# Two stacked models in float32: most token-to-feature tiles turned by VectorE block transposes and a bounce through a scratch array, in place of TensorE and transposing DMAs

## The reference

```
h   = mlstm_chunkwise(q, k, v, i_pre, log_f)          # 8 heads, matrix memory
y_a = headnorm(h * sigmoid(o)) * g * silu(z_a)
xc  = causal_dwconv(xb, lru_conv_w) + lru_conv_b
r,i = sigmoid(xc @ w_a + b_a), sigmoid(xc @ w_x + b_x)   # blocks of 256x256
log_a = -8 * r * softplus(-lam)
h_t = exp(log_a) * h_(t-1) + xc * i * sqrt(1 - exp(2 * log_a))
y_b = h * silu(z_b)
x   = x + concat(y_a, y_b) @ w_out
```

## Time and profile before

| | |
|---|---|
| median of 3 runs | 3274.63 us (3273.33 to 3274.72) |
| span of the profiled execution, first to last instruction | 3271.3 us |
| its own time beside the span | its span and about 3.3 us around it, by the median |
| TensorE clock granted | 1.000 |
| PE busy | 3257.1 us (100%), 15142 matmuls |
| DVE busy | 2082.9 us (64%) |
| ACT busy | 1830.6 us (56%) |
| POOL busy | 174.0 us (5%) |
| DMA | 637.77 MB, mean 195 GB/s |
| queue of the weight loads | 59.2% of 16 engines' span |

### The profile page before, as it was taken

The page is one execution under the profiler, slowest core; times in us unless marked ns, Lnnn a source line. Parts: engine busy times, 40 slices in busy tenths (PEclk is TensorE's granted clock), DMA queues, the critical chain, the costliest instruction groups (busy, mean ns, idle before and its releaser), DMA issues.

```text
span 3271.3 us, 39485 instructions
## 1 busy us (share of the span) xinstructions
PE 3257.1 (100%) x15142; PEld 2708.7 (83%) x15142; DVE 2082.9 (64%) x2843; ACT 1830.6 (56%) x2394; POOL 174.0 (5%) x241
## 2 busy tenths in 40 slices
PE   9999999999999999999999999999999999999999
PEld 7888888888888888888888888888888888888887
DVE  6558655756757755657667565665555667757664
ACT  5555545546665455546665565555556555565553
POOL 2000000000000000000000000000000321200000
PEclk9999999999999999999999999999999999999999
DMA  8666666565566666565567666556656565575565
GB/s 274 211 205 196 200 194 187 191 192 176 181 208 197 192 195 197 183 201 174 186 211 228 189 206 193 183 176 190 193 185 207 173 183 181 191 228 188 180 198 174
DMA packets 395740, 637.77 MB, mean 195 GB/s; under 512 B 102108, under 2 KB 104484, under 8 KB 395168
## 3 DMA queue, kind: packets, MB, share of 16 engines
q1 hardware_dynamic: 382928, 601.50, 59.2%
q0 software_dynamic: 10336, 27.45, 2.7%
q10 hardware_dynamic: 2288, 6.30, 0.5%
HBM read 608.10 MB, written 6.62 MB: 188 GB/s over the span
## 4 chain that ended last, share of the span: by engine, by line
PE 94%; ACT 2%; DVE 2%; DMA 1%; issue 1%; SPq 0%; ACTq 0%
PE acc L1727 29%; PE acc L1729 29%; PE acc L1728 29%; DVE weights_lo L1272 1%; PE tr L1814 1%; ACT weights_hi L946 1%; PE nm L1917 1%; ACT work L1012 1%; PE tr L1796 0%; PE tr L1727 0%; ACT work L1005 0%; PE tr L1729 0%; PE tr L1905 0%; PE tr L1728 0%; SPq L768 0%
## 5 line engine op out<-in xcount | busy, mean ns | idle before, releaser
L1272 DVE TENSOR_TENSOR weights_lo<-weights_raw,weights_hi 128x1024 fp32r<-128x1024 f32 x1103 | 1340.6, 1229 | 953.3 <-ACT weights_hi L946 950.0
L946 ACT ACTIVATE weights_hi<-weights_raw 128x1024 fp32r<-128x1024 f32 x1103 | 1156.0, 1057 | 1003.4 <-PE acc L1729 919.1
L1727 PE MATMUL acc<-weights_hi,u_hi 128*128 128x512 f32 x3136 | 1237.5, 395 | 0.0
L1729 PE MATMUL acc<-weights_hi,u_lo 128*128 128x512 f32 x3136 | 1222.6, 390 | 0.0
L1728 PE MATMUL acc<-weights_lo,u_hi 128*128 128x512 f32 x3136 | 1221.4, 389 | 0.0
L1727 PEld LDWEIGHTS acc<-weights_hi,u_hi 128*128 128x128 f32 x3136 | 588.9, 188 | 124.7 <-issue 4.0
L1729 PEld LDWEIGHTS acc<-weights_hi,u_lo 128*128 128x128 f32 x3136 | 588.5, 188 | 123.6
L1728 PEld LDWEIGHTS acc<-weights_lo,u_hi 128*128 128x128 f32 x3136 | 589.0, 188 | 119.3
L1727 PE MATMUL acc<-weights_hi,y_hi 128*128 128x512 f32 x1280 | 501.6, 392 | 0.9 <-DVE y_lo L1276 0.3
L1729 PE MATMUL acc<-weights_hi,y_lo 128*128 128x512 f32 x1280 | 498.6, 390 | 0.0
L1728 PE MATMUL acc<-weights_lo,y_hi 128*128 128x512 f32 x1280 | 498.2, 389 | 0.0
(11 more groups left out here) (285 smaller groups left out, 1957.7 us busy)
## 6 DMA issues: line engine op xcount, KB each, us to landing
weights_raw<-in_w_in_dram SPq DMA_DIRECT2D x384, 512.0 KB, 3.9
weights_raw<-in_w_out_dram SPq DMA_DIRECT2D x256, 512.0 KB, 4.4
weights_raw<-in_a_w_in_dram SPq DMA_DIRECT2D x176, 512.0 KB, 4.2
weights_raw<-in_b_w_in_dram SPq DMA_DIRECT2D x112, 512.0 KB, 3.7
weights_raw<-in_c_w_in_dram SPq DMA_DIRECT2D x112, 512.0 KB, 4.3
weights_raw<-in_w_mem_kv_dram SPq DMA_DIRECT2D x63, 512.0 KB, 5.1
kv_scratch<-work ACTq DMA_DIRECT2D x8, 512.0 KB, 5.3
qk_tiles<-in_w_a_dram POOLq DMA_DIRECT2D x8, 512.0 KB, 4.4
```

What stands on the lines that cost most here:

```text
L946: SC_E.activation(WH[:, b % RING], RAW[:, b % RING], ACT.Copy).then_inc(sem("hi_done"), 1)
L1272: V.tensor_tensor(WL[:, b % RING], RAW[:, b % RING], WH[:, b % RING].bitcast(F32), ALU.subtract).then_inc(sem("lo_done"), 1)
L1727: T.matmul(dst, hi_l, hi_r, start=start, stop=False, **kw)
L1729: return T.matmul(dst, lo_l, hi_r, start=False, stop=stop, **kw)
```

## The change

A turn is now: one DVE instruction transposes all 32x32 blocks of the 256x512 tile (128x1024 elements) into a buffer (piece `flip`); POOL stores that buffer to a scratch array in HBM with four DMAs, one for each 32 partitions, in pieces of 1 KB; three slots later (`fetch`) POOL waits for the four stores and loads the array back as 128 rows of 4 KB, with features on partitions and the tokens of each feature in runs of 32. What reads the tile takes it in that order.

All tiles but 15 take this way: 81 turns (37 of `xbar`'s kind, now `bounce`; 8 q, 8 xb, 8 z_b, 20 queries and keys). Still turned by PE are the memory's four tiles, the first four of x, the fourth tile of x at five layer ends, and the third group of kinds B and C. There are five scratch arrays (lanes), each shared by buffers that aren't in use together. `apart`, the transposing DMAs, `ct` and `cz` are gone. `join` reads the fetched tile directly (four ACT instructions, of 256 elements), `low` is eight DVE instructions of 128 with a gain, or four without, and comes one slot behind `join` instead of two.

Slots move with it. Counted from the end of its chunk, a q or xb tile is flipped at once, joined at +5, convolved at +6 and +7; the gates of the LRU come at +10 and +11 (before: about +6 and +7 from the second round on), the scans at +16 (before +12), `lrz` 8 and `lry` 10 slots behind the z_b chunk (before 5 and 7). `qt` comes 6 slots behind the chunk instead of 3; attention starts at `h - 1` instead of `h - 3` or `h - 4`, the memory's two or three slots later; `ya` is flipped 6 slots behind its z_a chunk (before, taken apart or turned at 8).

```diff
-ISSUE, JOIN, LOW = 7, 5, 2
+FETCH, JOIN, LOW = 3, 5, 1
+LANE = {"u0": "uq", "q": "uq", "a0": "uq", "u1": "um", "m": "um", "x": "xz", "z": "xz", "n": "n",
+        "a": "ab", "b": "ab"}
...
-    def apart(slot, src, ready, buf):
-        q = pl.piece(slot, "apart", src=src, ready=ready, buf=buf)
-        pl.piece(slot + ISSUE, "turn", at=q, buf=buf)
+    def turn(slot, src, ready, buf):
+        q = pl.piece(slot, "flip", src=src, ready=ready, buf=buf)
+        pl.piece(slot + FETCH, "fetch", at=q, buf=buf)
         return q
+    def bounce(slot, src, ready, dst, kt0, gain, buf):
+        q = turn(slot, src, ready, buf)
+        p = pl.piece(slot + JOIN, "join", dst=dst, kt0=kt0, gain=gain, at=q, buf=buf)
+        pl.piece(slot + JOIN + LOW, "low", at=p, buf=buf)
+    def keys_in(hn, **kw):
+        q = turn(pl.here() + 1, "n", ("hn_out", hn), "n")
+        pl.piece(pl.here() + 6, "qt", at=q, buf="n", **kw)
...
+            q = turn(pl.here(), "xt", ("cq_x", cq), "q")
+            pl.piece(pl.here() + 5, "cjoin", at=q, buf="q")
+            for r in range(2):
+                pl.piece(pl.here() + 6 + r, "conv", to="cq", r=r, l=l, taps=QC + 4 * j)
+            pl.piece(pl.here() + 8, "cqs", j=j)
...
-            ya.append(tp(s + 8, "o", ("mf_out", mf), "y", 12, gain) if p == 3 else
-                      xbar(s + 8, "o", ("mf_out", mf), "y", 4 * p, gain, "m"))
+            ya.append(bounce(s + 6, "o", ("mf_out", mf), "y", 4 * p, gain, "m"))
...
-            pl.piece(pl.here() + 1, "ct", to="cx", at=cx)
+            q = turn(pl.here(), "xt", ("cx_x", cx), "x")
+            pl.piece(pl.here() + 5, "cjoin", at=q, buf="x")
...
-            c += 4 if p == 0 else 2
+            c = pl.here() + 7
...
-            pl.piece(pl.here() + 3, "cz", at=zb)
-            pl.piece(pl.here() + 5, "lrz", l=l, p=p)
-            lr.append(pl.piece(pl.here() + 7, "lry", l=l, p=p))
+            q = turn(pl.here(), "xt", ("zb_out", zb), "z")
+            pl.piece(pl.here() + 8, "lrz", l=l, p=p, at=q)
+            lr.append(pl.piece(pl.here() + 10, "lry", l=l, p=p))
...
-            tm = attention("mem", 3, pl.here() - NB + 4)
+            tm = attention("mem", 3, pl.here() - NB + (6 if kind == "A" else 7))
...
-                ts.append(attention(kind, grp, h - 3 if kind == "B" else h - 4))
+                ts.append(attention(kind, grp, h - 1))
...
+        SPILL = {lane: nc.dram_tensor("turn_scratch_" + lane, [4, 32, 4, 256], F32).ap()
+                 for lane in LANES}
...
+                    if k == "flip":
+                        wait(pool, "flipped", p)
+                        for a in range(4):
+                            pool.dma_start(SPILL[LANE[p.buf]][:, :, a].rearrange("b r e -> r b e"),
+                                           flipped(p.buf)[32 * a:32 * a + 32].rearrange("p (b e) -> p b e", b=4)
+                                           ).then_inc(sem("spilled_" + LANE[p.buf]), 16)
+                    elif k == "fetch":
+                        pool.wait_ge(sem("spilled_" + LANE[p.buf]), 64 * (p.nth + 1))
+                        pool.dma_start(turned(p.buf), SPILL[LANE[p.buf]].rearrange("b r a e -> (b r) (a e)")
+                                       ).then_inc(sem("fetched_" + LANE[p.buf]), 16)
...
+                    elif k == "flip":
+                        ref(dve, p.ready)
+                        if p.nth:
+                            dve.wait_ge(sem("fetched_" + LANE[p.buf]), 16 * p.nth)
...
+                        V.transpose(flipped(p.buf).rearrange("p (b q s) -> p q b s", b=4, q=8), src
+                                    ).then_inc(sem("flipped"), 1)
...
                     elif k == "qt":
-                        wait(act, "qt_pe", p)
+                        act.wait_ge(sem("fetched_n"), 16 * (p.at.nth + 1))
...
                     elif k == "lrz":
-                        for j in range(2):
-                            z = ZT[:, 2 * j:2 * j + 2]
-                            i = stt(z, z, 1.0, TR[:, j].rearrange("p (a b) -> p a b", b=256), ALU.add, ALU.mult)
+                        for t in range(2):
+                            for f in range(4):
+                                z = tokens(ZT, t)[:, f]
+                                i = stt(z, z, 1.0, by_token("z", t)[:, f], ALU.add, ALU.mult)
```

244 lines of the change are left out of this document (98 added, 146 removed).

## The result

The changed kernel takes 3533.14 us (median of 4 runs, 3530.86 to 3555.03) beside 3274.47 for the kernel before (4 runs): a ratio of 1.0804 [1.0785, 1.0822], 259 us slower. The forecast was 3318, its range 3256 to 3352. The direction was right and the size was off by a factor of six: +44 forecast, +259 measured.

The account below looks back on a forecast made before the run. PE, busy 3257.1 of 3271.3 us, was taken to bound the kernel; 81 us of new waits (38 + 8 + 10 + 19 + 6) less 37.4 saved gave +44, so 3318 us, range 3256 to 3352.

Parts of the forecast that it names:

- L = 9.1: Each turn, from the end of DVE's transpose to the data's return: 9.1 us, ends 8.0 and 11.
- PE saves 37.4: On PE, 42 of 44 transposed tiles go, at 0.89 us each: 37.4 us saved.
- Stores 3.0, fetch 4.1: Within a turn, a 128 KB store lands in 3.0 us and the fetch takes 4.1 us.
- DMA load at nothing, up to 5 us: 81 x 1 MB moved, 85 MB or 13% more traffic; costs nothing, up to 5 us if landing slows.
- LRU 38: LRU stage, four rounds per layer: DVE's burst and the x turn make PE wait 38 us in two layers.
- q tiles 8: q tiles: the loop through one buffer runs late, 4.2 us per layer with gate rows, 8 in all (4 to 16).
- Last `ya` 10: Last `ya` tile of a layer: ready about 5 us after w_out's block needs it, 10 us in two layers.
- Keys in B and C 19: Attention in kinds B and C: normalization and turns at head groups cost 9.6 us in each kind, 19 in all.
- The lead covers 5.6 us: Weight blocks: a DVE or ACT burst making `weights_lo` up to about 5.6 us late costs nothing.
- rivals, 1 and 4: 1: lead hides the waits, 3237 or 3255 to 3265, chance 0.25. 4: waits cancel the saving, 3275, chance 0.10.
- Rival 3: POOL's DMA issues wait for DVE instructions, lengthening each turn by about 5 us: about 3408 us; chance 0.04.
- Rival 2: The turn is dearer, by a 2.4 us transpose or stores landing in over 4 us: 3349 to 3383; chance 0.11.

Follow-up runs that it names:

- in_place: Changed kernel without the turns' stores and loads, so readers take the DVE-transposed buffer as it stands: 3286.96 us, ratio 1.0035.
- in_place_traffic: Changed kernel with all stores and loads issued, loads going to a spare array, readers taking the transposed buffer without waiting: 3332.21 us, ratio 1.0173.

## Why the prediction was wrong

The step that failed is the sum's term **L = 9.1**, which measured 13.4, and with it the end of 11 that the range was made from; and a term was left out, **the clock**. New waits were 201 us, not 81, the clock cost 78, not 0, and the broken overlap of matmuls some 14 by the estimate above: 120 + 78 + 14 = 212 of the miss of 215. Of the 201, 33 are there in in_place and 30 more in in_place_traffic, by PE's idle time (47.1 and 77.2 us); the 138 that are left come with L. So the traffic and the issues, priced at nothing, are a second part of the step. (Waits below are counted from the usual 0.227 us between starts, so each holds 0.16 us of this overlap.)

- *PE saves 37.4.* Right: L1814's 208 and 104 transposes and L1796's 144 became 120, and PE's busy time fits the saving (-37.4 + 78 + 14, measured +59.8).
- *Transpose 1.22, issue 0.53.* Right (1.236, 0.558).
- *Stores 3.0, fetch 4.1.* Wrong: 5.2 for the fourth store, and 5.8. 3.0 is right for the first store of a turn (2.9) and for every store from SP (2.8 to 3.1); what was priced at nothing is the company of three others on POOL's queue, which the rows of a single 8 KB store and of 16 KB loads don't show. The upper end of 11 was built from the same rows. The fetch was taken below its nearest row (4.4); why it needs 5.8 stays open; it is not POOL's queue, since one from SP beside the same stream needs as long (5.1 to 6.9).
- *DMA load at nothing, up to 5 us.* Wrong: in_place_traffic puts 45 on traffic and issues together, and ACT's waits for weight loads went from 63.8 to 216.6 us. The forecast named these waits as a sign that it would be wrong. Its 39 us for them are two of the five arrays, which are all that the earlier trace rows shows; its 85 MB leave out what the transposing DMAs no longer move, so that the total grew by 64 MB, 10% and not 13%.
- *LRU 38.* Measured 42 (20.1 and 21.9 a layer; gate matmuls 2.4 to 2.85 late for 2.4, the block behind the scans 3.0 for 3.5, since `lrz` took 2.97 for 3.65, the tail 4.1 for 4.75). Right in its places and sizes: the block behind the scans and the tail wait as long in in_place, at L = 0, so they are DVE's burst, as forecast. But L was 12.8 there (transpose's end to `cjoin`, 779.16 to 791.94 in the second round). The 3.7 more did not show; PE itself came later, by 11 us of lower clock per stage (0.05 x 221.8), 2.8 a round. That this is what hid them is argued, not tested. Rounds took 59.6 and 57.9 us between `x` transposes, for a forecast of 55.
- *q tiles 8.* Measured 34. With 4.3 more of L in each of three loops the same walk gives 4.2 + 12.9 = 17.1 a layer, 34 in two. That it fits so well is in part luck: in_place, with L = 0, waits 4.1 a layer in the same stretch, which the walk doesn't have, and 4.6 are the gate rows, which wait for weights behind POOL's stores and not for a q tile. Kind A's memory query fits by L alone: 6 forecast, 14 measured, 2 x (2.9 + 4.3) = 14.4.
- *Last `ya` 10.* Measured 29 with the rest of the v, o and z_a chunks. The two waits for the last tile's `y_lo` are 7.9 and 7.8 of it: 16 where 10 were forecast, a little less than two times 4.3 more. The other 13 stand at `weights_lo` of blocks before, where the forecast had none; what held those up was not traced.
- *Keys in B and C 19.* Measured 70 (28 and 42). Six late points times 4.3 and the 19 give 45. The remaining 25 are most likely the bias loads behind POOL's stores in kind C, where in_place_traffic is 20 longer than in_place; that is argued, not separated. The forecast put `fc` there, and did not name the bias loads. *Memory keys 0*: measured 7.
- *The lead covers 5.6 us.* It holds where DVE is late once. A join that waits on ACT holds up the three splits behind it, and the lead is used up at once: "behind it stand the next split" was written of DVE's transpose and not of ACT's join, the one that waits longest.

Of the rivals, 1 and 4 fall by the time itself, and in_place, with L = 0, is still not faster. Rival 3 falls, although L did grow by about the 5 us that it priced: the 281 issues with DVE busy for over 90% of them took 0.559 us in the mean, the 69 with DVE busy for under 10% 0.557, and the longest of all 0.62; nor do the stores of a turn land later where DVE is busier, but for the first of the four, by 0.2 us. Of the rule of the Trainium skill behind it ("SBUF — State Buffer", "Who interferes with whom") this says only that it did not bite here; whether any DVE instruction of this kernel is of the two-port kind, no run shows. Rival 2, the dearer turn, is the nearest in kind; its reason, stores that land in over 4 us, came true for the third and fourth of a turn, and its 3349 to 3383 was too low for the same two reasons, L above 11 and the clock.

## What to carry to other kernels

Price a round trip through DMAs by rows of transfers of its own size, issuer and company, and where there are none, let the upper end be twice the sum: here 9.1 became 13.4, and the time went from a small loss to 8%. Look on each in-order engine for what stands behind the instruction that waits for the data: it was ACT's join, and the weight splits behind it, that turned a late tile into a late weight stream. Add the clock to every forecast of long PE waits: 201 us of waits brought some 80 more at the lower clock. And look on the issuing queue too for what stands behind a turn's stores: here the gates' weights and the bias loads did.

## What the hardware showed unexpectedly

- A 128 KB store in 1 KB pieces landed in 3.2 to 4.7 us (medians of the scratch arrays) from POOL and 2.6 to 3.2 from SP; four in a row from POOL needed 2.9, 3.9, 4.6 and 5.2, four from SP 2.8 to 3.1 each; a 512 KB fetch in 5.0 to 6.9 from POOL, where all DMAs together moved 199 GB/s.
- A turn by 16 direct moves inside SBUF took 6.5 to 7.0 us (medians) when SP and POOL shared the issues, 12.9 when POOL issued them all: each landing rose from 2.0 to 3.9 us, and the last issue came 8.2 us behind the transpose.
- Half clock was granted for 198 us, in 36 stretches, each behind a wait of PE, in a kernel with PE busy for 94% of the span; PE worked in 156 of them.
